# Attention's pairs of heads as a software pipeline: the copy of the turned pair ahead of the next exponential, probabilities divided before they are turned, outputs written feature-major

## What is computed

```python
def block(qblk):
    s = jnp.einsum('bqkgd,blkd->bkgql', qblk, k, preferred_element_type=jnp.float32)
    p = jax.nn.softmax(s, axis=-1).astype(v.dtype)
    return jnp.einsum('bkgql,blkd->bqkgd', p, v)
```

## Time and profile before

| what | value |
|---|---|
| median of 3 runs | 2071.72 us (2070.91 to 2073.83) |
| profiled execution, its own time | 2072.51 us |
| its span | 2070.7 us |
| PE busy | 1916.3 us, 93% of the span |
| DVE, ACT, POOL busy | 48%, 34%, 30% |
| the stretch around attention | about 906 us to 1117 us of the span |
| share of PE in the chain that ended last | 79% |

### The profile page before, as it was taken

How to read it: one execution, slowest core, us unless ns; L and a number is a source line. 1 busy time by engine, 2 the same in 40 slices (tenths; PEclk the granted TensorE clock), 3 DMA queues, 4 the chain that set the end, 5 groups by cost and what they waited for, 6 DMA issues and landing times.

```text
span 2070.7 us, 43615 instructions
## 1 busy us (share of the span) xinstructions
PE 1916.3 (93%) x18272; PEld 1760.2 (85%) x18272; DVE 991.5 (48%) x1544; ACT 702.1 (34%) x1208; POOL 615.5 (30%) x337
## 2 busy tenths in 40 slices
PE   6899888999999996999998998989797999999996
PEld 3765778999999995878877887878696999999996
DVE  5497625442144416845545666666535444134422
ACT  4111424442144423236433332323234443134421
POOL 2200244443344453211111111111054444334452
PEclk8999998999999998999998999999898999999998
DMA  8766331222122221110110000000021222122221
GB/s 334 276 243 235 144 110 41 81 75 84 65 71 71 86 69 45 51 64 31 41 57 2 3 3 3 3 3 3 7 72 43 79 71 90 63 71 71 89 70 65
DMA packets 35344, 159.67 MB, mean 77 GB/s; under 512 B 3936, under 2 KB 4448, under 8 KB 28560
## 3 DMA queue, kind: packets, MB, share of 16 engines
q1 hardware_dynamic: 32832, 152.02, 20.7%
q10 hardware_dynamic: 1872, 3.61, 0.5%
q0 software_dynamic: 512, 2.13, 0.3%
HBM read 154.73 MB, written 3.01 MB: 76 GB/s over the span
## 4 chain that ended last, share of the span: by engine, by line
PE 79%; DVE 9%; ACT 4%; issue 3%; POOL 2%; DMA 2%; SPq 0%; DVEq 0%; POOLq 0%; PEldq 0%; ACTq 0%; PEld 0%
PE ps L218 17%; PE ps L220 17%; PE ps L219 17%; PE ps L1830 10%; PE ps L1869 2%; PE ps L1459 2%; PE ps L665 2%; PE ps L655 2%; PE ps L1809 2%; PE ps L359 2%; DMA arena<-in_mod_w 1%; DVE arena L553 1%; PE ps L1155 1%; ACT arena L1510 1%; POOL w_lo L257 1%
## 5 line engine op out<-in xcount | busy, mean ns | idle before, releaser
L218 PE MATMUL ps<-h_hi,w_hi 128*128 128x320 f32 x1632 | 513.1, 314 | 52.9 <-POOL h_lo L534 48.3
L257 POOL TENSOR_TENSOR w_lo<-wslot,w_hi 128x1024 fp32r<-128x1024 f32 x130 | 320.1, 2463 | 702.3 <-ACT w_hi L252 702.3
L219 PE MATMUL ps<-h_lo,w_hi 128*128 128x320 f32 x1632 | 509.1, 312 | 0.0
L220 PE MATMUL ps<-h_hi,w_lo 128*128 128x320 f32 x1632 | 508.9, 312 | 0.0
L218 PEld LDWEIGHTS ps<-h_hi,w_hi 128*128 128x128 f32 x1632 | 310.4, 190 | 63.9 <-issue 45.1
L219 PEld LDWEIGHTS ps<-h_lo,w_hi 128*128 128x128 f32 x1632 | 310.9, 190 | 0.1
L220 PEld LDWEIGHTS ps<-h_hi,w_lo 128*128 128x128 f32 x1632 | 310.7, 190 | 0.0
L252 ACT ACTIVATE w_hi<-wslot 128x1024 fp32r<-128x1024 f32 x130 | 138.0, 1062 | 485.3 <-PE ps L220 425.2
L1012 DVE SCALAR_TENSOR_TENSOR arena<-arena,par 128x641 f32<-128x641 f32 x88 | 125.2, 1423 | 339.5 <-ACT arena L987 339.5
L1830 PE MATMUL ps<-arena 64*64 64x64 f32 (+2 forms) x5760 | 243.3, 238 | 16.4 <-DVE arena L2137 12.6
L1830 PEld LDWEIGHTS ps<-arena 64*64 64x64 f32 x5760 | 215.9, 136 | 31.4 <-DVE arena L2137 16.7
(11 more groups left out here) (198 smaller groups left out, 2888.3 us busy)
## 6 DMA issues: line engine op xcount, KB each, us to landing
arena<-in_mod_w SPq DMA_DIRECT2D x48, 1024.0 KB, 6.5
wslot<-in_ffn_up SPq DMA_DIRECT2D x88, 512.0 KB, 3.4
wslot<-in_ffn_down SPq DMA_DIRECT2D x32, 704.0 KB, 4.1
wslot<-in_cd_w SPq DMA_DIRECT2D x22, 512.0 KB, 3.5
wslot<-in_w_out SPq DMA_DIRECT2D x16, 512.0 KB, 3.5
wslot<-in_ab_w SPq DMA_DIRECT2D x12, 512.0 KB, 7.6
x<-in_x_fm SPq DMA_DIRECT2D x2, 1280.0 KB, 7.3
out_y<-arena ACTq DMA_DIRECT2D x8, 320.0 KB, 2.4
```

The source lines that it names most:

```text
L218: nc.tensor.matmul(out, wh[:, m], hi[:, kk, t], start=(kk == 0), stop=False)
L219: nc.tensor.matmul(out, wh[:, m], lo[:, kk, t], start=False, stop=False)
L220: last = nc.tensor.matmul(out, wl[:, m], hi[:, kk, t], start=False, stop=(kk == k_all - 1))
L257: pool.tensor_tensor(wl[:, :], wslot[:, s, 0:tile_cols[base]], wh[:, :], ALU.subtract).then_inc(lo_ready, 1)
```

## The change

The diff does four things.

1. **Division early.** `norm(n)` on DVE (reciprocal, and a multiply of the whole row of probabilities in SBUF) stands between exponential and transposes; `turn(n)` waits for it (`p_ready`) instead of for the exponential. `out(n)` becomes one plain copy of 128x128.
2. **Feature-major output.** In `output(n)` values are the weights (64 columns) and the turned probabilities the moving operand (128 columns). Head 0 writes PSUM partitions 0 to 63 and head 1 writes 64 to 127, taken alternately.
3. `turn_output` and `turned` are gone.
4. **Another order.** ACT does `copy(n)` and then `expo(n + 1)`; DVE does `norm(n)`, `out(n - 1)`, `biggest(n + 1)`; PE's loop is rotated. The last `out` stands behind `a_b_r(0)`, and the scan's start waits for `o_used` of 19 pairs, not of 20.

```diff
@@ PE
-                pe.wait_ge(e_ready, 2 * n + 2)
+                pe.wait_ge(p_ready, 2 * n + 2)
...
-                for e in range(2):
-                    values = [vd[:, 0, vcols]] if t == 0 else lat + [cv[:, vcols]] if e == 0 else [cv[:, vcols]] + lat
-                    for b, v in enumerate(values):
-                        last = nc.tensor.matmul(middle(n, P + HD * e, P + HD * e + HD), probT[:, e, b, :], v, start=(b == 0),
-                                                stop=(b == len(values) - 1))
+                values = [[vd[:, 0, vcols]]] * 2 if t == 0 else [lat + [cv[:, vcols]], [cv[:, vcols]] + lat]
+                for b in range(len(values[0])):
+                    for e in range(2):
+                        last = nc.tensor.matmul(middle(n, P, 2 * P)[HD * e:HD * e + HD, :], values[e][b], probT[:, e, b, :],
+                                                start=(b == 0), stop=(b == len(values[0]) - 1))
...
             for n in range(PAIRS):
-                turn(n)
-                if n <= TILES_END:
-                    half(halves_before(n))
...
-                output(n)
-                score(n + 2)
+                if n:
+                    output(n - 1)
+                score(n + 1)
...
+                turn(n)
+                if n <= TILES_END:
+                    half(halves_before(n))
-            turn_output(BLOCKS - 1)
+            output(PAIRS - 1)
@@ ACT
-                copy(n)
...
-                expo(n + 2)
...
+                copy(n)
+                expo(n + 1)
...
-            turned(BLOCKS - 1)
@@ DVE
+            def norm(n):
+                dve.wait_ge(e_ready, 2 * n + 2)
+                w = P if n % NT == 0 else T
+                for e in range(2):
+                    st(nc.vector.reciprocal(srow[:, prob_slot(n, e), 2:3], srow[:, prob_slot(n, e), 1:2]))
+                for e in range(2):
+                    slot = prob_slot(n, e)
+                    st.wait(but=1 - e if e == 0 else 0)
+                    nc.vector.tensor_scalar(prob[:, slot, 0:w], prob[:, slot, 0:w], srow[:, slot, 2:3], None, ALU.mult).then_inc(p_ready, 1)
+
             def out(n):
...
+                nc.vector.tensor_copy(ycat1[:, KA + blk, t * P:(t + 1) * P], middle(n, P, 2 * P)).then_inc(o_used, 1)
...
-                out(n)
-                biggest(n + 2)
+                norm(n)
+                if n:
+                    out(n - 1)
+                biggest(n + 1)
...
             ahead.a_b_r(0)
+            out(PAIRS - 1)
@@ PE, first unit of the scan
-            pe.wait_ge(yt_used, BLOCKS)
-            pe.wait_ge(o_used, PAIRS)
+            pe.wait_ge(o_used, PAIRS - 1)
```

More of the change, by code:

```diff
@@ L1354, in prob_slot @@
             return 2 * (n % 2) + e
-        EXTRAS = (9, 11, 13)
+        EXTRAS = (10, 12, 14)
         TILES_END = 15
         def halves_before(n):
-            return 2 + n + sum(2 for e in EXTRAS if n > e)
+            return 2 + n + sum(2 for e in EXTRAS if n >= e)
         def complete(n):
             return halves_before(n) // 2
-        SUM_AFTER = {1: 0, 3: 1, 5: 2, 7: 3}
-        TURN_AT = {17: 0, 18: 1, 19: 2}
+        SUM_AT = {2: 0, 4: 1, 6: 2, 8: 3}
         def attn_pe(pe):
@@ L1403, in key_sums @@
                 head_sums(pe, ksq[m % 2], 0).then_inc(ksum_ready, 1)
-            def turn_output(blk):
-                if blk == 0:
-                    wait(emptied["act"], entry[-1, "rate", 1][2])
-                else:
-                    pe.wait_ge(yt_used, blk)
-                pe.wait_ge(o_used, NT * (blk + 1))
-                for t in range(NT):
-                    last = nc.tensor.transpose(ps[:, t // 4, t % 4 * P:(t % 4 + 1) * P], ycat1[:, KA + blk, t * P:(t + 1) * P], ident)
-                last.then_inc(yt_ready, 1)
             def score(n):
@@ L1467, in attn_pe @@
             for n in range(PAIRS):
-                turn(n)
-                if n <= TILES_END:
-                    half(halves_before(n))
+                if n:
+                    output(n - 1)
+                score(n + 1)
+                if n in SUM_AT:
+                    key_sums(SUM_AT[n])
+                if n in EXTRAS:
+                    half(halves_before(n) - 2)
+                    half(halves_before(n) - 1)
                 if n == TILES_END + 1:
@@ L1531, in key_root @@
                 warm(act, ACT.Exp)
-            def turned(blk):
-                act.wait_ge(yt_ready, blk + 1)
-                nc.scalar.activation(ycat1[:, KA + blk, :], ps[:, 0:2, :].rearrange("p a b -> p (a b)")[:, 0:T],
-                                     ACT.Copy).then_inc(yt_used, 1)
             wait = Waits(act)
@@ L1598, in biggest @@
                     ins.then_inc(max_ready, 1)
+            def norm(n):
[7 more added lines that the diff above has]
+                    nc.vector.tensor_scalar(prob[:, slot, 0:w], prob[:, slot, 0:w], srow[:, slot, 2:3], None, ALU.mult).then_inc(p_ready, 1)
             def out(n):
                 blk, t = n // NT, n % NT
-                dve.wait_ge(e_ready, 2 * n + 2)
-                for e in range(2):
-                    st(nc.vector.reciprocal(srow[:, prob_slot(n, e), 2:3], srow[:, prob_slot(n, e), 1:2]))
                 dve.wait_ge(o_ready, n + 1)
-                st.wait()
-                for e in range(2):
-                    ins = nc.vector.tensor_scalar(ycat1[:, KA + blk, t * P + HD * e:t * P + HD * e + HD],
-                                                  middle(n, P + HD * e, P + HD * e + HD), srow[:, prob_slot(n, e), 2:3], None, ALU.mult)
-                ins.then_inc(o_used, 1)
+                nc.vector.tensor_copy(ycat1[:, KA + blk, t * P:(t + 1) * P], middle(n, P, 2 * P)).then_inc(o_used, 1)
             def key_root(m, begin):
@@ L1618, in attn_dve @@
             biggest(0)
-            biggest(1)
-            taps(0)
             for n in range(PAIRS):
-                out(n)
-                biggest(n + 2)
-                if n % 2 and n <= TILES_END:
-                    taps(complete(n))
+                norm(n)
+                if n:
+                    out(n - 1)
+                biggest(n + 1)
+                if n == 0:
+                    taps(0)
+                if n and n % 2 == 0 and n <= TILES_END + 1:
+                    taps(complete(n - 1))
                 if n in EXTRAS:
-                    taps(complete(n) + 1)
-                if 2 <= n < 2 + 2 * KA:
-                    key_root(n // 2 - 1, 2 * (n % 2))
-                if n == TILES_END:
+                    taps(complete(n) - 1)
+                if 3 <= n < 3 + 2 * KA:
+                    key_root((n - 3) // 2, 2 * ((n - 3) % 2))
+                if n == TILES_END + 1:
                     st.wait()
@@ L1959, in unit @@
                 need((UNITS.index((o, 0)), "Vt", 1))
+                wait(o_used, PAIRS)
                 wait(step_read, STEPS_READ * n)
```

37 lines of the change are left out of this document (13 added, 24 removed).

## The result

The changed kernel takes 2047.74 us (median of four, 2046.88 to 2049.43), the kernel before, run beside it, 2072.26 (2070.91 to 2073.83): a ratio of 0.9884, with an interval of 0.9871 to 0.9896. Forecast were 2048 us and a range of 2040 to 2061. The profiled execution has a span of 2045.8 us and took 2047.58 us itself, where the one of the kernel before took 2072.51.

The account below looks back on a forecast made before the run. PE's own work was taken to bound attention beside half tiles, and the PE, ACT and DVE chain plus low clock its tail. -13 - 14 + 3.5 = -23.5 us gave 2048 us, range 2040 to 2061.

Parts of the forecast that it names:

- waits that go: Beside half tiles, about 4 of the 8.1 us that outputs waited for copies go; 3 us of new waits come.
- one fall of the clock: In the tail, one stretch at half speed adds 3.5 us; bounds 0, and 7 for two.
- The output products: In attention, narrow alternating products take 1.3 us per latent output, saving 1.0 us each; context outputs save nothing.
- The rival that the strips don't overlap: In attention's outputs, products for the two heads gain no overlap, 2.3 + 0.2 us each: 2061 us; chance 0.14.
- The part with half tiles: Pairs 0 to 15, bound by PE's own work: 12 us of output work and 1 us of net waits go, 13 us less.
- the slower rival: In eight turns with `taps`, DVE becomes what PE waits for: up to 29 us more, 2077 us; chance 0.04.
- The division: On DVE, 2 x 0.49 us a pair, 16 us in all, free beside half tiles except where DVE's work meets.
- The tail: Pairs 16 to 19, bound by the chain through PE, ACT and DVE: 29.1 instead of 43 us, 14 us less.
- the rival that POOL holds up the division: DVE's multiply is held by POOL's low parts, half of 11 tiles at 1.5 us: +8, 2056 us; chance 0.08.

Follow-up runs that it names:

- the heads one after the other: Against the changed kernel, each head's output products stand together, head 0 then head 1, instead of alternating: 2056.67 us, ratio 0.9923.
- Splitting the keys' work: Against the changed kernel, DVE's rate step and first half of the scan's key work moved one loop earlier: 2047.59 us, run again 2044.53 us.

## Why the prediction was right, step by step

The terms are right in kind and mostly in size: less work for the outputs, waits that go, a shorter chain in the tail, one fall of the clock. That the median came within 0.3 us of 2048 is partly luck. In the profiled execution attention gained 26.2 us where 23.5 were forecast; 1.7 of that was lost ahead of it, where nothing was changed. In the second trace of the same kernel the part gained 11.9 us instead of 15.1, and the forecast of 13 lies between.

**The output products.** 1.3 us were forecast, 1.24 measured; a latent output saves 1.03 us, twelve of them 12.4. The nearest rows, products in narrow tiles that alternate, were the right price. A context output of four records takes 0.37 us (1060.92 to 1061.29), so sixteen more records cost 0.87, 0.054 each, and some 0.15 us lie on top in either; the half tile's last product costs 0.24 us ahead of an output instead of 0.15, so that an output with its step is 1.33 us. The Trainium skill (TensorEngine Tiling (Array Packing), Key Properties) has TensorE drained at a change of tiling mode; a cost of this kind agrees with it. The rival that the strips don't overlap is what the heads one after the other show, 2056.67 us. It is not quite the row that I had priced it by: 0.0975 us for each record, changes of shape and all, instead of 0.114 and 0.2 us more.

**The part with half tiles.** Forecast -13, measured -15.1 us. Of waits, 3.6 us of outputs went (forecast 4), and 2.4 us came at the score and the turn (forecast 3). The size is near, the pattern is not. I had four pairs with 0.6 us each and 1 us at the first; there are 1.56 us at the first and a single other wait of 2.32, in a context pair. The rows of DVE, POOL and PE there (timeline):

```profile
1003.99 4.21 DVE L1561 SCALAR_TENSOR_TENSOR arena<-arena 128x128 f32<-128x128 f32 x4 [4.52 <-ACT arena L1487]
...
1004.99 2.41 POOL L257 TENSOR_TENSOR w_lo<-wslot,w_hi 128x1024 fp32r<-128x1024 f32 x1 [7.58 <-ACT w_hi L252]
...
1008.13 2.15 DVE L1598 RECIPROCAL arena<-arena 128x160 f32<-128x160 f32 x2
...
1010.34 1.01 DVE L1587 TENSOR_SCALAR arena<-arena 128x640 f32<-128x640 f32 x2
1011.27 0.28 DVE L1592 COPY arena<-ps 128x128 f32<-128x128 f32 x1
...
1011.61 0.71 PE L1428 MATMUL ps<-arena 128*128 128x128 f32 x4 [2.32 <-DVE arena L1592]
```

The token shift takes 4.21 us beside POOL's low part instead of 2.05, and the roots stand behind it, while PE has only a turn of 2 and an output of 4 records to spend: my count took the PE work of a latent pair and the DVE work without POOL. These are the two ends that the slower rival needed together, and they met once, not in eight pairs. The wait at the first pair is POOL's as well: DVE's small product there takes 1.85 us instead of 0.28 beside a low part, and the division and `out` stand behind it.

```profile
918.94 1.85 DVE L1576 TENSOR_TENSOR arena<-arena 128x1 f32<-128x1 f32 x2
918.30 2.41 POOL L257 TENSOR_TENSOR w_lo<-wslot,w_hi 128x1024 fp32r<-128x1024 f32 x1 [3.99 <-ACT w_hi L252]
```

Outputs and waits as I had counted them make 13.9 of the 15.1 us. The rest is the 2.2 us that the eight waiting outputs cost beside their idle time, less 1.1 for the dearer step into twelve narrow outputs. I had taken a wait to cost what the trace calls idle, and it costs more.

**The division.** Forecast to be free beside half tiles, except where all of DVE's work meets: it costs 1.6 us there, out of 17.5 us of DVE. That holds for one division. Doubled, it adds 6.2 us of waits there, and the clock is lower besides. The cover is thus used up within 1 us more a pair, and DVE's share of busy time (63% in the part) did not tell that.

**The tail.** Forecast 29.1 at the full clock and 3.5 for the clock, 32.6; measured 31.7. By terms: to the start of turn 17 it is 11.3 us (forecast 11.5, by 4.7 and 8.0 less a turn of 1.2), the loop before turn 18 is 6.4 (6.7), that before turn 19 is 7.9 (6.6), from turn 19 to the scan it would be 3.9 at the full clock (4.3, with 0.3 for `a_b_r` that never showed), and the clock costs 2.2 (3.5). The third was too small by 1.3 us for a reason that can be seen (DVE and POOL of the changed kernel):

```profile
1084.18 2.29 DVE L1587 TENSOR_SCALAR arena<-arena 128x640 f32<-128x640 f32 x2
1084.34 1.79 POOL L2284 TENSOR_TENSOR arena<-wslot 128x640 f32<-128x640 f32 x1 [4.01 <-ACT wslot L1992]
```

The division takes 2.29 us instead of 1.02 and ends soon after POOL does. It is the mechanism of the rival that POOL holds up the division, in one place and not in eleven tiles. The Trainium skill (GPSIMD Engine Reference, Specifications) names contention of POOL with VectorE instructions in a two-port mode, besides those with two inputs; this row, with one input, agrees with it, though no row tells an instruction's mode. Splitting the keys' work takes the two apart: the division is 1.02 us again, and a product with two inputs is the one that takes 2.16.

The clock fell once, for some 10 us, as long as the longer of the two falls before; 7.5 us of it lie in the tail and 2.7 in the scan's first products. In the tail it cost only 2.2 us (the turn 2.40 for 1.25, the output 2.33 for 1.24), since PE waited for the rest of it: the 3.5 us were at half speed for 7 us of work that isn't there. In the tail's sum the third loop and the clock thus miss by 1.3 us each and cancel, which is luck too.

**What acted on what.** The order alone brings 14.8 us in attention, products and early division alone 18.5; the whole change 26.2 and not 33.3. In the tail -8.5 and -9.2 make -11.1: both shorten one chain. With the products alone the outputs wait 10.0 us for copies, where the kernel before has 4.5 and the whole change 5.6, so much of the work that PE is spared there comes back as waits. The clock has a share that I can't separate: its mean in the tail is 0.80 before, 0.87 with the order alone, 0.80 with the products alone and 0.88 with both. In the part they nearly add. There the one with the products has a fall of the clock at 922 us, worth about 1.6; without it -6.3 and -10.9 make -15.1, and the score's wait, which each alone brings to 2.6 and 2.3 us, comes to 3.9 with both.

## What to carry to other kernels

Price a product in a new shape by the rows that are like it in tile and in alternation, not by its old shape: 64-column products for two strips are worth 0.062 us a record when they alternate and 0.0975 when they don't. Work that an idle engine takes on is free only where something else is the later of the two; read it for each stretch, and beside what else runs, since 17.5 us of DVE cost 1.6 in the part with half tiles and 3.7 in the tail, and the same work once more 18.3, part of it by the low clock. In a loop without slack, look at what stands in one engine's queue ahead of what the other waits for: a copy of 0.28 us behind a division of 1 us cost 0.95 and 0.75 us in the two loops of the tail. And count a wait that goes as more than its idle time, here 0.27 us more.

## What was not expected of the hardware

The granted clock falls at different places in executions of one program: two falls of 3.4 us from 921 and 1010 us in one trace of the changed kernel and none in the other, with spans that agree within 0.2 us. Each began behind a wait of PE of 1.56 us or 2.31 us, and the same waits stood in the trace without falls. A comparison of stretches between two traces is thus uncertain by 1.6 us for each fall inside; the same stretch of several traces, or the fall's own windows, must be looked at first.

The medians of one kernel on two chips lay 3.1 us apart (2047.59 and 2044.53), with no overlap of eight runs, while the kernel before moved by 0.6 us (2071.8 and 2072.46). Whether chip or chance made the difference is open.
